# Score matmuls ahead of the later tasks' row-maximum pieces in TensorE's attention slots

## The chip, the cores and the metric

The kernel runs on one core of one Trainium2 chip. The metric is the device time of one execution in microseconds (us), the median of the runs shown. Lower is better.

## The reference, cut to what matters

One transformer block over 1024 positions of width 1024, all in float32. A normed input is projected once. Four branches mix the positions: a gated short convolution, sparse attention, causal pooling and a spatial gating unit. Their outputs are gated and merged, an output projection and a residual follow, and a gated feed-forward layer with a short convolution ends the block. The change lies in the attention branch. Cut to that branch, for each tile of 128 queries:

```python
sc = einsum('bqgrd,bngd->bqgrn', qb, kc) * scale      # compressed keys (63 of them)
pc = softmax(where(cval, sc, NEG));   o_c = pc @ vc
ss_ = einsum('bqgrd,bqgkd->bqgrk', qb, ksel) * scale  # selected blocks: all 16 are selected here
ps = softmax(where(smask, ss_, NEG)); o_s = ps @ vsel
sw = einsum('bqgrd,bkgd->bqgrk', qb, kwb) * scale     # window of the last 512 positions
pw = softmax(where(wmask, sw, NEG));  o_w = pw @ vwb
o = gt[..., 0:1] * o_c + gt[..., 1:2] * o_s + gt[..., 2:3] * o_w
```

There are 8 heads of 64 channels in 2 groups of 4 heads. The heads of a group share keys and values. The top 16 of 16 key blocks are taken, so the selected branch is plain causal attention.

## The kernel before, in words

The kernel is one program with five instruction streams (SyncE for the transfers, GpSimd, ScalarE, VectorE, TensorE), written out by hand and tied together by counting semaphores. Nothing reorders the work: each engine executes what its block in `build` issues, in that order. After the input norm, a loop over the two groups (`GROUPS`) does first the projection of q, k and v for eight tiles of 128 positions and then the attention of the group. The other branches, the merges, the output projection and the feed-forward layer follow, all of them built from 128x512 matmuls with operands split into a high and a low part (L1617 to L1619, L1765).

**Tasks, units and pieces.** `attention_tasks` makes 24 tasks per group: tiles 7 down to 0, and for each tile one task of kind "slc", one "win", one "cmp". A task's keys are cut into units of 128 keys (`units`, 74 in a group). The softmax of a query needs its row maximum first, and that maximum is computed by a pass of its own. `attention_pieces` cuts each task's score rows into pieces of at most 512 columns (77 in a group). For a piece, TensorE's `rows` computes rough scores with the queries on the partitions: one 128-row matmul for each head (L1519), followed by a short bf16 matmul that adds the mask where the piece holds a diagonal or a window edge or is of kind "cmp" (L1521). The pieces alternate between banks 0 and 1, so `rows` waits until VectorE has reduced the piece before the last (`max_done`). VectorE takes the maximum (L1095, written to `nmx`); for a task with over 512 keys it joins two halves (L1100). When the last piece of a task is reduced, GpSimd builds `shift`, a diagonal matrix of the negated maxima (L627).

**Units.** `scores` computes a unit with the keys on the partitions and all four heads in 512 columns: high keys (L1541), low keys (L1542), a mask where needed (L1544) and the broadcast of the maxima (`ones` against `shift`, L1546). It waits for `shift` at the first unit of a task, and for the exponential of the unit before the last (`exp_done`). ScalarE then makes `pT` by Exp (L753) and its high part (L756), VectorE the low part `pT_l` (L1087), and `values` multiplies with the values, three matmuls with 65-column weights (L1562 to L1564), in a slot that is `LAG` = 3 later.

**After a task's last unit.** ScalarE evacuates the sum (`oT`, L762), TensorE turns it (L1590, slot "turn"), and VectorE divides and gates it (`wtmp`, L1114; `wgt`, L1118; `o_gated`, L1121). After the third task of a tile GpSimd adds the three branches (L636, L638, slot "sum"), TensorE transposes the result (L1599, slot "final"), and ScalarE and VectorE write it as a high and a low part (L767, L1129).

**Slots.** `attention_slots` lays this out in 81 slots, one unit each. It places a piece up to `MAXIMA` - 1 = 3 tasks and up to `LEAD` = 12 positions ahead. Slot 0 holds the eight pieces of task 0, slot 11 holds nine (tasks 2 and 3), and most others hold none, one or two. All four compute engines walk the same list `slots`, each with its own order inside a slot. VectorE's order: the reductions of the slot's pieces, the low part of the unit of the slot before, the work of a turn, the work of a final. ScalarE's: exponential and high part, evacuation, final. GpSimd's: the shift of a task whose last piece stands in the slot, then a sum. TensorE's order inside a slot, which the change touches, is at L1569 to L1603: a step of the key compression in slots 0 to 3, 6 and 10, then `rows` for all pieces, `scores`, `values`, turn, final.

Of the kernel before, what the change touches and what calls it, by code (L numbers as in the profile page):

```python
# [101 lines left out]
def after(eng, semaphore, base, n):  # L102


    if n > 0:
        eng.wait_ge(semaphore, base + n)
# [71 lines left out]
def build(nc, x, norm1_g, w_in, conv_a_w, qk_norm_g, cmp_pe, cmp_w1, cmp_w2, pool_w, pool_scale,  # L178
# [13 lines left out]
    with ExitStack() as ctx:  # L192
# [1218 lines left out]
        def _(pe):  # L1411
# [19 lines left out]
            with pe.Fori(0, GROUPS) as g:  # L1431
# [41 lines left out]
                def compressed(step, part=None):  # L1473

                    if step == 0:
                        if part == 0:

                            pe.wait_ge(cbias_done, g + 1)

                        j = part // 2  # L1480
                        for l in range(part % 2 * (L16 // 2), (part % 2 + 1) * (L16 // 2)):
                            ins = nc.tensor.matmul(bank[0:HD, 7, j * HD:j * HD + NCMP], w1[:, j, l, :],
                                                   kcT[:, j, l:l + CMP_STRIDE * (NCMP - 1) + 1:CMP_STRIDE],
                                                   start=l == 0, stop=l == L16 - 1)
                    elif step == 1:

                        pe.wait_ge(compress_act, g * 3 + 1)
                        pe.wait_ge(const2_loaded, 32)
                        pe.sem_inc(passed, 1)
                        for j in range(2):  # L1490
                            ins = nc.tensor.matmul(bank[0:NCMP, 7, 256 + j * HD:256 + (j + 1) * HD], h1[:, j, 0:NCMP],
                                                   w2[:, j, :], start=True, stop=True)
                    else:
                        pe.wait_ge(compress_dve, g * 3 + 3)
                        pe.sem_inc(passed, 1)
                        for a in range(2):
                            ins = nc.tensor.transpose(bank[:, 7, 384 + a * CW:384 + a * CW + NCMP],
                                                      ckd[0:NCMP, a, :, :].rearrange("n u d -> n (u d)"), ident[0:NCMP,
                                                              0:NCMP])
                    if part is None or part == 3:  # L1500
                        ins.then_inc(compress_pe, 1)

                def rows(at, n, r0, heads, c, w):


                    i, kind, k0, keys, blocks = tasks[n]
                    after(pe, max_done, g * PIECES, at - 1)
                    masks = []
                    if kind == "cmp":
                        masks.append((0, CW, cmask[:, i, :]))  # L1510
                    else:
                        if kind == "win" and i >= WIN // P and c == 0:
                            masks.append((0, P, wstart[:, :]))
                        if c + w == keys:
                            masks.append((w - P, P, tri[:, :]))
                    for r in range(heads):
                        o = bank[:, at % 2, r * w:(r + 1) * w]
                        kh = kcAB[:, 0, :] if kind == "cmp" else kAB[:, 2 * (kind == "win"), k0 + c:k0 + c + w]
                        ins = nc.tensor.matmul(o, qT[:, r0 + r, i * P:(i + 1) * P], kh, start=True, stop=not masks)  # L1519
                        for m, (a, mw, mask) in enumerate(masks):  # L1520
                            ins = nc.tensor.matmul(o[:, a:a + mw], identb[:, :], mask, start=False, stop=m == len(masks) - 1)  # L1521
                    ins.then_inc(rows_done, 1)

                def scores(u, n, j):

                    i, kind, k0, keys, blocks = tasks[n]
                    if j == 0:
                        pe.wait_ge(shift_done, g * NT + n + 1)
                    after(pe, exp_done, g * UNITS, u - 1)
                    q = qT[:, :, i * P:(i + 1) * P]  # L1530
                    if kind == "cmp":
                        pe.sem_inc(passed, 1)
                        nr, kh, kl, mask = CW, kcAB[:, 0, :], kcAB[:, 1, :], cmask[:, i, :]
                    else:
                        nr, at = P, k0 + j * P
                        kh, kl = (kAB[:, 2 * (kind == "win") + a, at:at + P] for a in range(2))
                        mask = tri[:, :] if j == blocks - 1 else None
                        if kind == "win" and i >= WIN // P and j == 0:
                            mask = wstart[:, :]
                    o = bank[0:nr, 3 + u % 2, :]  # L1540
                    nc.tensor.matmul(o, kh, q, start=True, stop=False)  # L1541
                    nc.tensor.matmul(o, kl, q, start=False, stop=False)  # L1542
                    if mask is not None:
                        nc.tensor.matmul(o, mask, identb[:, :].unsqueeze(1).broadcast_to([P, REP, P]), start=False,  # L1544
                                stop=False)
                    nc.tensor.matmul(o, ones[:, 0:nr], shift[:, n % MAXIMA, :, :], start=False,  # L1546
                            stop=True).then_inc(s_done, 1)

                def values(u, n, j):

                    i, kind, k0, keys, blocks = tasks[n]
                    pe.wait_ge(ptl_done, g * UNITS + u + 1)
                    if j == 0:
                        after(pe, evac_done, g * NT, n - 1)
                    pe.sem_inc(passed, 1)
                    if kind == "cmp":
                        nr, vh, vl = CW, vc_h[:, :], vc_l[:, :]
                    else:
                        ty = 0 if kind == "slc" else 1
                        nr, vh, vl = P, v_h[:, ty, k0 // P + j, :], v_l[:, ty, k0 // P + j, :]  # L1560
                    o = bank[0:HD + 1, 5 + n % 2, :]
                    nc.tensor.matmul(o, vh, pT_h[0:nr, u % RING, :], start=j == 0, stop=False)  # L1562
                    nc.tensor.matmul(o, vh, pT_l[0:nr, u % RING, :], start=False, stop=False)  # L1563
                    nc.tensor.matmul(o, vl, pT_h[0:nr, u % RING, :], start=False, stop=j == blocks - 1).then_inc(pv_done, 1)  # L1564
# [5 lines left out]
                for slot in slots:  # L1570
                    if slot["n"] <= COMPRESS[0]:
                        compressed(0, slot["n"])
                    elif slot["n"] in COMPRESS:
                        compressed(COMPRESS.index(slot["n"]))
                    if slot["n"] == COMPRESS[2] + 1:
                        pe.wait_ge(compress_act, g * 3 + 3)
                    for piece in slot["pieces"]:
                        rows(*piece)
                    if slot["unit"]:
                        scores(*slot["unit"])  # L1580
                    if slot["values"]:
                        values(*slot["values"])
                    if slot["turn"] is not None:

                        n = slot["turn"]
                        pe.wait_ge(evac_done, g * NT + n + 1)
                        after(pe, gated, g * NT, n)
                        pe.sem_inc(passed, 1)
                        for r in range(REP):
                            ins = nc.tensor.transpose(bank[:, 7, r * (HD + 1):(r + 1) * (HD + 1)],  # L1590
                                                      oT[:, n % 2, r * P:(r + 1) * P], ident[0:HD + 1, 0:HD + 1])
                        ins.then_inc(turned, 1)
                    if slot["final"] is not None:

                        i = slot["final"]
                        pe.wait_ge(summed, g * TT + i + 1)
                        after(pe, ol_done, g * TT, i)
                        for b in range(2):
                            ins = nc.tensor.transpose(bank[:, 2, b * P:(b + 1) * P],  # L1599
                                                      o_gated[:, 3 * i % 4, b * P:(b + 1) * P], ident[:, :])  # L1600
                        ins.then_inc(final_done, 1)
# [204 lines left out]
```

## Time and profile before

| what | us |
|---|---|
| median of 3 runs | 2223.41 |
| lowest and highest of them | 2220.38, 2224.12 |
| span of the profiled execution, first to last instruction | 2220.0 |
| TensorE matmul busy in it | 2124.8 (96%) |
| VectorE, ScalarE, GpSimd busy | 1001.7, 668.0, 108.5 |
| mean granted TensorE clock | 0.974 |
| attention slots of group 0, of group 1 (from the first row piece to the last transpose) | 126.9 to 308.9, 397.7 to 580.4 |

The profile is of one execution, on one core. The record of it gives its span and no total of its own beside it; the nearest total is the lowest run, 0.4 us above the span. Times in the rows are microseconds from the span's start. A matmul's duration in a timeline is its start to its modelled end and overlaps the next one's, so the pace is read from start to start. "PEld" is the loading of weights, which runs beside the matmuls. "PEclk" is the share of the full TensorE clock (2.4 GHz) that was granted: 1.00 or 0.50, or a mean of both over a stretch.

### The profile page before, as it was taken

What the parts mean: (1) busy time and instruction counts of PE and PEld (TensorE: products, weight loads), DVE (VectorE), ACT (ScalarE), POOL (GpSimd) and SP (SyncE); (2) the same over time, 40 slices, a digit from 0 to 9 for tenths busy, and PEclk for the clock granted to TensorE, in tenths of its full rate; (3) what the DMA queues carried; (4) which work ended last, traced back from release to release, by engine and by line L of the source; (5) the groups of instructions that cost most, each with busy time, mean ns of one, the idle gap of its engine ahead of it and who ended that gap; (6) DMA issues with size and microseconds to landing.
All of it is one profiled execution on the core that took longest, in us unless ns stands there. A gap on an engine that the chain in (4) does not pass through costs nothing.

```text
span 2220.0 us, 27176 instructions
## 1 busy us (share of the span) xinstructions
PE 2124.8 (96%) x10106; PEld 1717.7 (77%) x10106; DVE 1001.7 (45%) x1543; ACT 668.0 (30%) x970; POOL 108.5 (5%) x109
## 2 busy tenths in 40 slices
PE   4989979799899999999999999999999999999998
PEld 3956659566588888888788888878888888888886
DVE  6647756477323323234533432544443444344443
ACT  4446644466422111122312322422111122111111
POOL 1002320023100000000000000000000000000000
PEclk6979989799999999999999999999999999999999
DMA  6010000000112111121211111502111111101111
GB/s 167 1 39 1 1 17 1 1 1 1 30 43 57 48 53 43 43 62 43 57 48 52 29 53 51 171 1 86 42 35 57 47 47 57 57 28 47 54 41 76
DMA packets 148135, 99.03 MB, mean 45 GB/s; under 512 B 22203, under 2 KB 139661, under 8 KB 148045
## 3 DMA queue, kind: packets, MB, share of 16 engines
q1 hardware_dynamic: 147805, 97.07, 14.9%
q8 instruction: 54, 0.88, 0.2%
q0 software_dynamic: 240, 0.79, 0.1%
q14 instruction: 36, 0.29, 0.0%
HBM read 93.64 MB, written 4.19 MB: 44 GB/s over the span
## 4 chain that ended last, share of the span: by engine, by line
PE 92%; DVE 4%; ACT 2%; issue 2%; POOL 1%; DMA 0%; SPq 0%; DVEq 0%; ACTq 0%; POOLq 0%; PEldq 0%
PE bank L1617 18%; PE bank L1618 18%; PE bank L1619 18%; PE bank L1765 11%; PE bank L1719 4%; PE bank L1519 2%; PE bank L1541 2%; PE bank L1546 1%; PE bank L1562 1%; PE bank L1542 1%; PE bank L1564 1%; PE bank L1563 1%; PE bank L1456 1%; PE bank L1460 1%; PE bank L1458 1%
## 5 line engine op out<-in xcount | busy, mean ns | idle before, releaser
L1617 PE MATMUL bank<-actT_h,ring_h 128*128 128x512 f32 x1536 | 599.4, 390 | 8.8 <-DVE actT_l L1353 4.8
L1619 PE MATMUL bank<-actT_h,ring_l 128*128 128x512 f32 x1536 | 598.5, 390 | 0.0
L1618 PE MATMUL bank<-actT_l,ring_h 128*128 128x512 f32 x1536 | 598.4, 390 | 0.0
L1617 PEld LDWEIGHTS bank<-actT_h,ring_h 128*128 128x128 f32 x1536 | 288.8, 188 | 69.9 <-issue 7.8
L1619 PEld LDWEIGHTS bank<-actT_h,ring_l 128*128 128x128 f32 x1536 | 288.7, 188 | 60.0
L1618 PEld LDWEIGHTS bank<-actT_l,ring_h 128*128 128x128 f32 x1536 | 288.8, 188 | 59.4
L1136 DVE TENSOR_TENSOR ring_l<-raw,ring_h 128x1024 fp32r<-128x1024 f32 x128 | 156.4, 1222 | 353.0 <-ACT ring_h L783 352.7
L783 ACT ACTIVATE ring_h<-raw 128x1024 fp32r<-128x1024 f32 x128 | 134.7, 1053 | 142.1 <-PE bank L1619 124.8
L1365 DVE TENSOR_TENSOR x<-x,bank 128x1024 f32<-128x1024 f32 x88 | 107.4, 1221 | 100.7 <-PE bank L1765 99.5
L940 ACT ACTIVATE ffa_h<-ffc 128x1024 fp32r<-128x1024 f32 x22 | 23.3, 1061 | 341.4 <-DVE ffc L1397 341.4
L753 ACT ACTIVATE pT<-bank 128x512 f32<-128x512 f32 (+1 forms) x148 | 88.1, 595 | 117.6 <-PE bank L1546 114.0
L1095 DVE TENSOR_REDUCE nmx<-bank 128x1 f32<-128x512 f32 (+4 forms) x154 | 95.5, 639 | 60.7 <-PE bank L1521 47.1
L1087 DVE TENSOR_TENSOR pT_l<-pT,pT_h 128x512 fp32r<-128x512 f32 (+1 forms) x148 | 104.4, 706 | 24.9 <-ACT pT_h L756 24.7
L1765 PE MATMUL bank<-wd_h,ffa_h 128*128 128x512 f32 x352 | 109.3, 392 | 3.7 <-DVE ffa_l L1399 3.7
L1765 PE MATMUL bank<-wd_l,ffa_h 128*128 128x512 f32 x352 | 108.9, 391 | 0.0
L1765 PE MATMUL bank<-wd_h,ffa_l 128*128 128x512 f32 x352 | 108.8, 391 | 0.0
L1617 PE MATMUL bank<-outb_h,ring_h 128*128 128x512 f32 x256 | 100.4, 392 | 2.5 <-DVE outb_l L1230 2.5
L1619 PE MATMUL bank<-outb_h,ring_l 128*128 128x512 f32 x256 | 100.4, 392 | 0.0
L1618 PE MATMUL bank<-outb_l,ring_h 128*128 128x512 f32 x256 | 100.2, 391 | 0.0
L756 ACT ACTIVATE pT_h<-pT 128x512 fp32r<-128x512 f32 (+1 forms) x148 | 93.5, 631 | 4.7
L1380 DVE TENSOR_SCALAR ffc<-ffg,chan 128x1024 f32<-128x1024 f32 x22 | 16.6, 754 | 163.4 <-ACT ffg L927 163.4
L627 POOL TENSOR_TENSOR shift<-ident,nmx 128x512 fp32r<-128x512 f32 x48 | 63.7, 1328 | 394.3 <-DVE nmx L1100 255.0
(303 smaller groups left out, 2993.2 us busy)
## 6 DMA issues: line engine op xcount, KB each, us to landing
raw<-in_w_in SPq DMA_DIRECT2D x60, 512.0 KB, 3.7
raw<-in_w_up SPq DMA_DIRECT2D x44, 512.0 KB, 3.9
wd_raw<-in_w_down SPq DMA_DIRECT2D x22, 512.0 KB, 5.2
raw<-in_w_branch SPq DMA_DIRECT2D x32, 256.0 KB, 2.7
x_in<-in_x SPq DMA_DIRECT2D x8, 512.0 KB, 8.1
raw<-in_w_o SPq DMA_DIRECT2D x8, 512.0 KB, 3.5
x<-in_x SPq DMA_DIRECT2D x8, 512.0 KB, 10.1
out<-x SPq DMA_DIRECT2D x8, 512.0 KB, 2.6
```

What stands on the lines that cost most here:

```text
L753: nc.scalar.activation(pT[0:nr, u % RING, :], bank[0:nr, 3 + u % 2, :], ACT.Exp).then_inc(exp_done, 1)
L756: nc.scalar.activation(pT_h[0:nr, u % RING, :], pT[0:nr, u % RING, :], ACT.Copy).then_inc(pth_done, 1)
L783: nc.scalar.activation(ring_h[:, slot, :], raw[:, slot, :], ACT.Copy).then_inc(ph_done, 1)
L1087: nc.vector.tensor_tensor(pT_l[0:nr, u % RING, :], pT[0:nr, u % RING, :], pT_h[0:nr, u % RING, :].bitcast(F32), ALU.subtract).then_inc(ptl ...
L1095: nc.vector.tensor_reduce(nmx[:, n % MAXIMA, c // HALF, r0:r0 + heads], bank[:, at % 2, 0:heads * w].rearrange("p (r n) -> p r n", r=heads ...
L1136: nc.vector.tensor_tensor(dst, src, hi.bitcast(F32), ALU.subtract).then_inc(pl_done, 1)
L1365: nc.vector.tensor_tensor(x2[:, t, :], x2[:, t, :], flat[:, (2 + t % 2) * 1024:(3 + t % 2) * 1024], ALU.add).then_inc(d_done, 1)
L1617: nc.tensor.matmul(o, wh(k), ah[:, k, cols], start=k == 0, stop=False)
L1618: nc.tensor.matmul(o, wh(k), al[:, k, cols], start=False, stop=False)
L1619: ins = nc.tensor.matmul(o, wl(k), ah[:, k, cols], start=False, stop=k == k_tiles - 1)
L1719: ins = nc.tensor.matmul(bank[:, first_bank + h, :], m, w[:, h * HALF:(h + 1) * HALF], start=k == 0 and n == 0, stop=k == KT - 1 and n == 2)
L1765: ins = nc.tensor.matmul(o[h], av, w[:, k, h * HALF:(h + 1) * HALF], start=k == 0 and n == 0, stop=k == 1 and n == 2)
```

## The change

In each slot, TensorE's list of pieces is parted in two. Pieces of the task that the slot's own unit belongs to stay ahead of `scores`. Pieces of a later task are issued after `scores` and ahead of `values`. The other engines' programs are unchanged, and so are the semaphores, the buffers and the instructions themselves.

```diff
@@ -1574,10 +1574,14 @@
                     if slot["n"] == COMPRESS[2] + 1:
                         pe.wait_ge(compress_act, g * 3 + 3)
+                    later = [p for p in slot["pieces"] if slot["unit"] and p[1] > slot["unit"][1]]
                     for piece in slot["pieces"]:
-                        rows(*piece)
+                        if piece not in later:
+                            rows(*piece)
                     if slot["unit"]:
                         scores(*slot["unit"])
+                    for piece in later:
+                        rows(*piece)
                     if slot["values"]:
                         values(*slot["values"])
                     if slot["turn"] is not None:
```

By the slot list, the eight pieces of slot 0 stay where they are (they are of task 0, as its unit is), and the other 69 pieces of a group, in 50 slots, move behind their slot's `scores`.

## Rows read from the trace of the kernel before

**Rows 1.** The page, part 1: busy time of each engine, share of the span, instructions.
```profile
PE 2124.8 (96%) x10106; PEld 1717.7 (77%) x10106; DVE 1001.7 (45%) x1543; ACT 668.0 (30%) x970; POOL 108.5 (5%) x109
```
**Rows 2.** A window of group 0's attention: length, busy time and instructions by engine, clock, DMA.
```profile
172.00:280.00 108.00, 107.31 (x578) 69.70 (x576) 79.03 (x160) 73.79 (x127) 32.04 (x27) 1.00 0.00 1
```
**Rows 3.** Waits of TensorE's matmuls, whole span: us in total, times, longest.
```profile
PE bank L1599 <- POOL o_gated L638: 8.0, 6, 2.8
...
PE bank L1541 <- ACT pT L753: 6.0, 2, 3.0
...
PE bank L1541 <- POOL shift L627: 4.2, 2, 2.1
...
PE bank L1519 <- DVE nmx L1095: 2.6, 12, 0.4
```
**Rows 4.** Timeline of VectorE in slot 11, group 0: start, us, instruction, idle before.
```profile
165.87 5.33 DVE L1095 TENSOR_REDUCE nmx<-bank 128x4 f32<-128x256 f32 x9 [1.43 <-PE bank L1521]
```
**Rows 5.** Timeline of TensorE at the start of slot 22, group 0.
```profile
193.01 0.40 PE L1519 MATMUL bank<-kAB,qT 128*128 128x512 f32 x1
193.24 0.23 PE L1521 MATMUL bank<-wstart,identb 128*128 128x128 bf16 x1
193.28 0.48 PE L1541 MATMUL bank<-qT,kAB 128*128 128x512 f32 x1
```
**Rows 6.** Lines L1541 and L1562: duration in ns, least, median, most.
```profile
L1541 PEld LDWEIGHTS bank<-qT,kAB x132: 186/200/354, 135.5 to 567.3; 128*128 128x128 f32 x132
L1541 PE MATMUL bank<-qT,kAB x132: 389/474/797, 135.5 to 567.3; 128*128 128x512 f32 x132
L1541 PEld LDWEIGHTS bank<-qT,kcAB x16: 135/148/153, 175.1 to 568.8; 128*64 128x64 f32 x16
L1541 PE MATMUL bank<-qT,kcAB x16: 387/424/430, 175.1 to 569.0; 128*64 128x512 f32 x16
...
L1562 PEld LDWEIGHTS bank<-pT_h,v_h x132: 134/136/229, 148.0 to 572.8; 128*65 128x65 f32 x132
L1562 PE MATMUL bank<-pT_h,v_h x132: 387/392/632, 148.2 to 572.8; 128*65 128x512 f32 x132
```
**Rows 7.** Timelines of three engines from slot 70 to the final of slot 71.
```profile
290.19 0.28 PE L1519 MATMUL bank<-kcAB,qT 128*128 128x64 f32 x1
...
290.82 0.43 PE L1541 MATMUL bank<-qT,kcAB 128*64 128x512 f32 x1
...
292.04 0.40 PE L1562 MATMUL bank<-pT_h,v_h 128*65 128x512 f32 x1
...
295.29 0.44 PE L1599 MATMUL bank<-ident,o_gated 128*128 128x128 f32 x2 [0.51 <-POOL o_gated L638]
...
291.48 0.42 DVE L1095 TENSOR_REDUCE nmx<-bank 128x4 f32<-128x256 f32 x1 [0.22 <-issue]
...
292.07 1.34 POOL L627 TENSOR_TENSOR shift<-ident,nmx 128x512 fp32r<-128x512 f32 x1 [3.27 <-DVE nmx L1095]
```
**Rows 8.** Timelines from slot 62 to the final of slot 64.
```profile
273.23 1.28 DVE L1095 TENSOR_REDUCE nmx<-bank 128x2 f32<-128x512 f32 x2
...
275.37 0.66 DVE L1118 TENSOR_TENSOR wgt<-wtmp,glog 128x4 f32<-128x4 f32 x1
...
274.67 1.34 POOL L627 TENSOR_TENSOR shift<-ident,nmx 128x512 fp32r<-128x512 f32 x1 [4.78 <-DVE nmx L1095]
...
278.87 0.33 PE L1599 MATMUL bank<-ident,o_gated 128*128 128x128 f32 x1 [0.69 <-POOL o_gated L638]
```
**Rows 9.** The sum and the final of tile 7 (slots 18 and 19).
```profile
187.21 1.06 POOL L638 TENSOR_TENSOR o_gated<-o_gated 128x256 f32<-128x256 f32 x1
...
188.58 0.38 PE L1599 MATMUL bank<-ident,o_gated 128*128 128x128 f32 x2
```
**Rows 10.** Windows of slots 11 to 13 in either group; columns as in Rows 2.
```profile
165.12:177.03 11.91, 10.98 (x53) 6.21 (x52) 10.46 (x20) 4.17 (x8) 2.49 (x2) 1.00 0.00 1
435.37:448.87 13.50, 12.56 (x53) 7.15 (x52) 10.30 (x20) 4.17 (x8) 2.49 (x2) 0.87 0.00 1
```

## The prediction

> **What bounds the kernel now.** I read four views, from coarse to fine. The page says that TensorE's matmuls are busy for 96% of the span and VectorE for 45% [rows 1], so the first question is whether the attention slots are different. The window over the middle of group 0's attention answers it: 107.31 us of matmuls in 108.00 us, at full clock, with VectorE at 79.03 and ScalarE at 73.79 us [rows 2]. Through most of the slots the path is TensorE's own list of matmuls. Giving another engine its input sooner can only pay where TensorE waits for that engine. The waits of the whole span name these places [rows 3]: 6.0 us for an exponential at L1541, 4.2 us for a shift at L1541, 2.6 us for the maxima at L1519, 8.0 us for GpSimd's branch sum at L1599. A difference under about 0.2% (4.4 us) can't be told from no change.
>
> **None of the waits that scores could shorten lies at a moved piece.** The 6.0 us for an exponential are two waits, one in each group. Both stand in slot 8, behind table loads and the compression steps on ScalarE, and slots 4 to 10 hold no piece. The two shift waits (4.2 us) are slot 0, whose eight pieces stay in front. So what the new order gives ScalarE, an exponential that starts earlier by the pieces' time, saves nothing: I cost it at 0, and what covers it is the dense list of TensorE. The waits for maxima stand in the runs of eight or nine pieces. In slot 11 VectorE reduces nine pieces in 5.33 us without a gap [rows 4], and TensorE follows it at that pace through two banks. With scores in front, the run starts later by the length of scores and ends later by the same, and the slot's sum of times is the same: 0. Neither order puts the scores inside the run. No instruction is added or dropped, no DMA is issued in these slots, and no wait is new; only the order of waits on TensorE differs.
>
> **Term 1, what follows a mask matmul.** A 512-column matmul starts 0.23 us before the next instruction [rows 5]. The short mask matmul after it starts only 0.04 us before L1541, but then L1541 lasts long: 474 ns in the median where a value matmul after a long one lasts 392 [rows 6]. The 82 ns are the loading of 128 weight columns, which a short matmul doesn't hide. Where the scores are of kind "cmp" and have 64 columns of weights, the load takes 148 ns, not 200, and the matmul 424, so 32 ns stick out [rows 6]. In the new order a masked piece is followed not by scores but by values, whose weights have 65 columns and load in 136 ns [rows 6]. By the nearest row (64 columns) that leaves 32 of 82 ns and saves 0.05 us. By the slot list, 31 slots of each group have a masked last piece, scores that aren't "cmp", and values that aren't either. That is 62 x 0.05 = 3.1 us saved. The bounds: nothing saved, if the values' first load sticks out as far as the scores' did (0), and all of it hidden, 62 x 0.082 = 5.1 us.
>
> What stood before the pieces (values, or the transposes of a turn) now stands before scores, with weights of the same 128 columns: 0. In the 7 slots of a group with "cmp" scores the saving is missing and a 128-column load follows their last matmul. I take 0.03 us each, 14 x 0.03 = 0.4 us lost, between 0 and 14 x 0.082 = 1.1 us. The eight slots of each group whose last piece has no mask, and slots 1 and 2 (no values yet): 0.
>
> **Term 2, later reductions.** What moves behind scores reaches VectorE later by the time of three score matmuls, 3 x 0.23 + 0.08 = 0.77 us. VectorE runs in order, so the low part and the turn's division queue behind the late reduction. The low part is needed three slots on; values have over 1.6 us in hand everywhere, by the timelines, and that covers it: 0. The tight chain is another: turn, division and gate on VectorE, sum on GpSimd, final on TensorE, within two slots. TensorE waits at three finals of each group, six times in all [rows 3]. The last stands behind all pieces and isn't touched. One by one, in group 0:
>
> - Final of slot 71. Its sum stands on GpSimd behind the shift of the last piece. That piece is computed from 290.19 to about 291.0 and reduced from 291.48, the shift starts at 292.07, and TensorE stands idle 0.51 us ahead of 295.29 [rows 7]. The "cmp" scores take 292.04 - 290.82 = 1.22 us [rows 7]. With them in front the piece ends at 292.2, is reduced from 292.3 instead of 291.48, and shift, sums and final come later by the same 0.85 us.
> - Final of slot 64. The reductions of slot 62 start at 273.23 because VectorE is free only then [rows 8]; with the pieces 0.77 us later they start at about 273.8. Then low part, division and gate: 0.6 us, on a final that already waits 0.69 us [rows 8].
> - Final of slot 19. The sum ends at 188.27, the final starts at 188.58 [rows 9], so 0.3 us are in hand. VectorE is about 0.35 to 0.4 us later after two turns in a row: 0.1 us.
> - The other finals have from 0.4 to 1.0 us in hand, or stand behind slots without pieces: 0.
>
> That is 1.55 us a group, 3.1 us in all. Lower bound: 0, if VectorE's lateness is made up. Upper bound: the full 0.77 us at all eight finals and 1.22 at slot 71's, less the 0.3 and more in hand, some 2.9 us a group, 5.8 us.
>
> Here a rule speaks against the change. In slot 62 VectorE's `wgt`, four values a partition, takes 0.66 us and ends at 276.03, and GpSimd's shift runs from 274.67 to 276.01 [rows 8]: the small one stood behind the big one. The Trainium skill says the same (SBUF — State Buffer, "Who interferes with whom"): a VectorE instruction with two SBUF inputs and a GpSimd instruction that reads SBUF take a shared port pair in turns, and the loser waits for the whole instruction. The trace agrees in this slot. Later shifts fall onto the gating more often by that rule, and the sum would be at the upper bound of term 2, not at 3.1.
>
> **Sum.** -3.1 + 0.4 + 3.1 = +0.4 us on the profiled execution (span 2220.0, no total of its own). It lies 0.4 us under the lowest run and 3.4 under the median, 2223.41; I put the difference on the median: 2223.8.
>
> **The rivals.** *Clock.* In group 1 the slots 11 to 13 take 13.50 us at a mean clock of 0.87, in group 0 11.91 at 1.00 [rows 10], same instructions. The nine paced pieces leave TensorE with gaps, and in group 1 it fell to half clock (1.2 GHz) behind them. The change moves dense scores from behind to ahead of the gaps, so either group can fall or not: -1.6 to +1.6 us, within the range, no sign. It widens each case.
>
> *Faster.* The mask term comes out at its bound (-5.1), the finals lose little because TensorE's savings and VectorE's catching up cancel (+1), and group 1 keeps its clock (-1.6): 2223.4 - 5.7 = 2217.7. For it: the weight loads of rows 6. Against it: the 64-column row shows 32 ns left, and rows 7 show a chain without any reserve. It needs over 4.4 us in all. 0.08.
>
> *Slower.* VectorE and GpSimd turn into the bound at the finals. Place: turn to final; price: the 0.77 us of scores at each final, 5.8 us in all as above. For it: rows 7 and 8, two finals with no reserve. Against it: four of the other finals have 0.4 us or more in hand. It decides if the mask term stays under about 1 us at the same time: +5.8 + 0.4 - 0.5 = +5.7, so 2229.1. 0.09.
>
> *The order doesn't change.* The slot list excludes it: 69 pieces of 77 move. 0.
>
> **How the numbers follow.** Forecast (mask term and finals cancel within 4 us): 0.83, all within 0.2%. Faster 0.08, slower 0.09. The range takes term 1 and term 2 against each other at about three quarters of their bounds, and 1.6 us of clock either way: -4 to +4 about 2223.6, so 2219.6 to 2227.8, and leaves out most of both rivals.
>
> **What would show it.** Steps: L1541 at 392 ns in the masked slots and L1562 at some 424; the final of slot 71 idle about 1.4 us and that of 64 about 1.3, in both groups; waits at L1541 and L1519 as before; the paced run of slot 11 as long as before, starting behind scores; L1599's waits at about 11 us in all instead of 8.0. I'd be wrong if L1562 after a mask stays at 392 (term 1 at its upper bound) or goes to 474 (no gain), if waits for `pT_l` turn up at L1562, or if all eight finals wait.

## The result, and the profile after

| | before | changed |
|---|---|---|
| median of the 20 runs of each, taken side by side, us | 2221.68 | 2224.57 |
| lowest to highest, us | 2220.11 to 2224.12 | 2222.46 to 2228.21 |
| ratio, 95% interval | | 1.0015 [1.0008, 1.0022] |
| span of the profiled execution, us | 2220.0 | 2224.0 (its own time: 2225.96) |

Two of the 20 runs before took 3466.93 and 3749.08 us; they are slow runs and are left out of the range shown, and the ratio is of fast runs.

The change costs 0.15%, some 3.3 us, by this ratio (2.9 us between the medians). That lies within the range given (2219.6 to 2227.8) and within the 0.2% called "no change", though the interval of the ratio excludes 1. Several lines moved down by four: L1590 is now L1594, L1599 is L1603.

The busy times of the page barely differ, so they explain nothing [rows 1]:

```profile
PE 2125.9 (96%) x10106; PEld 1718.5 (77%) x10106; DVE 1013.4 (46%) x1543; ACT 670.2 (30%) x970; POOL 107.8 (5%) x109
```

The waits of TensorE's matmuls, changed kernel (us in total, times, longest):

```profile
PE bank L1603 <- POOL o_gated L638: 11.8, 6, 2.8
PE bank L1541 <- ACT pT L753: 6.4, 4, 3.0
...
PE bank L1541 <- POOL shift L627: 4.2, 2, 2.1
...
PE bank L1519 <- DVE nmx L1095: 2.4, 11, 0.4
```

Against [rows 3] one line has moved by more than half a microsecond: the finals wait 11.8 us instead of 8.0, still six times. Waits for shifts are the same, those for maxima 0.2 us less, those for exponentials 0.4 us more. The 0.4 are two new waits of 0.19 us (at 150.80 in group 0), ahead of the 3 us wait of slot 8, and no wait for an exponential stands behind slot 8 in either kernel.

The two lines that answer to [rows 6], changed kernel (ns: least, median, most):

```profile
L1541 PEld LDWEIGHTS bank<-qT,kAB x132: 186/188/337, 135.7 to 571.6; 128*128 128x128 f32 x132
L1541 PE MATMUL bank<-qT,kAB x132: 389/397/795, 135.7 to 571.7; 128*128 128x512 f32 x132
...
L1562 PE MATMUL bank<-pT_h,v_h x132: 387/422/669, 148.3 to 577.2; 128*65 128x512 f32 x132
```

The first score matmul fell from 474 to 397 ns. The first value matmul, now the one behind the mask, rose from 392 to 422, not to 474. The same in slot 22, in TensorE's timeline (start, us, instruction), against [rows 5]:

```profile
196.07 0.40 PE L1546 MATMUL bank<-shift,ones 128*128 128x512 f32 x1
196.31 0.39 PE L1519 MATMUL bank<-kAB,qT 128*128 128x512 f32 x1
196.54 0.23 PE L1521 MATMUL bank<-wstart,identb 128*128 128x128 bf16 x1
196.58 0.43 PE L1562 MATMUL bank<-pT_h,v_h 128*65 128x512 f32 x1
196.84 0.39 PE L1563 MATMUL bank<-pT_l,v_h 128*65 128x512 f32 x1
```

Read the starts: from the mask (L1521, 196.54) to the second value matmul (196.84) it takes 0.30 us. In the kernel before, the same slot took 0.36 us from the mask to the second score matmul (193.24 in [rows 5] to 193.60):

```profile
193.60 0.40 PE L1542 MATMUL bank<-qT,kAB 128*128 128x512 f32 x1
```

The saving exists, at 0.05 to 0.06 us a slot. It can be added up over all masked pieces from slot 13 to slot 61 of group 0, 31 of them: from the start of the first matmul behind the mask to the next start it took 9.52 us in all before (medians 0.31 us for scores with 128 columns of weights) and 8.17 us in the changed kernel (0.26 for values). That is 1.35 us less.

What eats it is at the end of the group. Timelines around the final of slot 64, changed kernel:

```profile
280.99 0.44 PE L1603 MATMUL bank<-ident,o_gated 128*128 128x128 f32 x2 [1.27 <-POOL o_gated L638]
...
275.34 1.29 DVE L1095 TENSOR_REDUCE nmx<-bank 128x2 f32<-128x512 f32 x2 [0.43 <-PE bank L1521]
...
277.36 0.79 DVE L1118 TENSOR_TENSOR wgt<-wtmp,glog 128x4 f32<-128x4 f32 x1
...
276.79 1.34 POOL L627 TENSOR_TENSOR shift<-ident,nmx 128x512 fp32r<-128x512 f32 x1 [4.53 <-DVE nmx L1095]
```

In [rows 8] the reductions followed VectorE's own work without a gap; now VectorE waits 0.43 us for the pieces, everything behind them is late, and TensorE's idle time at the final is 1.27 us instead of 0.69. And from slot 68 to the final of slot 71:

```profile
291.80 0.40 PE L1564 MATMUL bank<-pT_h,v_l 128*65 128x512 f32 x1
292.18 0.44 PE L1594 MATMUL bank<-ident,oT 65*128 65x65 f32 x4
292.60 0.41 PE L1541 MATMUL bank<-qT,kcAB 128*64 128x512 f32 x1
...
293.78 0.19 PE L1519 MATMUL bank<-kcAB,qT 128*128 128x64 f32 x1
...
290.82 0.79 DVE L1118 TENSOR_TENSOR wgt<-wtmp,glog 128x4 f32<-128x4 f32 x1
291.65 0.42 DVE L1121 TENSOR_TENSOR o_gated<-bank,wgt 128x256 f32<-128x256 f32 x1
...
294.99 0.42 DVE L1095 TENSOR_REDUCE nmx<-bank 128x4 f32<-128x256 f32 x1 [1.50 <-PE bank L1521]
...
290.25 1.34 POOL L627 TENSOR_TENSOR shift<-ident,nmx 128x512 fp32r<-128x512 f32 x1 [2.34 <-DVE nmx L1095]
295.57 1.34 POOL L627 TENSOR_TENSOR shift<-ident,nmx 128x512 fp32r<-128x512 f32 x1 [3.98 <-DVE nmx L1095]
296.87 1.16 POOL L636 TENSOR_TENSOR o_gated<-o_gated 128x256 f32<-128x256 f32 x1
298.12 0.72 POOL L638 TENSOR_TENSOR o_gated<-o_gated 128x256 f32<-128x256 f32 x1
...
298.89 0.44 PE L1603 MATMUL bank<-ident,o_gated 128*128 128x128 f32 x2 [1.82 <-POOL o_gated L638]
```

Against [rows 7] the idle time ahead of the final grew from 0.51 to 1.82 us. A third place is new: in slot 69 the turn starts 0.38 us after L1564, not 0.23. It has to wait for the gating of slot 68, which ended only at 292.07. Its `wgt` took 0.79 us beside the shift (290.25 to 291.59), where the next one, with no shift beside it, took 0.16.

To compare kernels I cut each group at three matmuls that all versions have. "Slots 0 to 13" runs from the first row piece to the first value matmul of slot 13, "13 to 61" on to that of slot 61, "61 to 71" on to the final of slot 71. In us, worked out from the starts of matmuls, group 0 and group 1:

| kernel | slots 0 to 13 | 13 to 61 | 61 to 71 | to the last final |
|---|---|---|---|---|
| before | 49.41, 50.45* | 94.80, 94.79 | 24.15, 24.15 | 12.95, 12.93 |
| changed | 51.86*, 50.22* | 93.70, 93.68 | 26.15, 26.07 | 13.15, 13.01 |

The star (in the stages below too) marks a stretch in which the clock fell to half after it had risen; every group begins at half clock, until 138 to 141 us in group 0, before and after the change alike. The middle of a group gains 1.1 us, its end loses 2.0, in both groups alike. The third difference is the clock in slots 0 to 13. Windows over that part of group 0, first of the kernel before (columns as in Rows 2):

```profile
126.00:165.00 39.00, 31.81 (x151) 20.49 (x150) 18.05 (x40) 19.91 (x32) 2.49 (x2) 0.81 0.23 47
160.00:176.00 16.00, 13.79 (x66) 7.96 (x64) 13.19 (x32) 7.29 (x13) 2.49 (x2) 1.00 0.00 1
```

and of the changed kernel:

```profile
126.00:165.00 39.00, 33.06 (x146) 21.12 (x145) 17.38 (x39) 19.73 (x30) 2.49 (x2) 0.72 0.24 49
160.00:176.00 16.00, 15.25 (x55) 9.15 (x54) 10.90 (x27) 6.32 (x12) 2.48 (x2) 0.74 0.00 0
```

TensorE ran at half clock (1.2 GHz) for 6.8 us from 158.1 and for 3.4 us from 171.7; the kernel before had neither in this group. The first fall begins inside the 3 us wait for an exponential in slot 8, which both kernels have [rows 3]; that slot holds no moved piece. TensorE's timeline there, changed kernel:

```profile
159.04 0.79 PE L1541 MATMUL bank<-qT,kAB 128*128 128x512 f32 x1 [2.99 <-ACT pT L753]
```

The matmul behind the wait lasts 0.79 us instead of some 0.40, which is half clock in one row. The two profiles differ by 4.0 us of span: 2.4 in slots 0 to 13 of group 0, -0.2 in those of group 1, -2.2 in the middle stretches, +3.9 in the late ones, +0.3 in the tails, and -0.2 elsewhere. So the order itself makes +1.7 us in these two traces (-2.2 and +3.9).

### The profile page after: what moved, and what is told of

Same layout as the page of the kernel before. It is cut to its first block, busy times and chain, and to the rows that moved or that the text cites. A ratio compares the mean times of both kernels' runs of the same rounds, so it can differ in the third digit from the quotient of the medians.

```text
span 2224.0 us, 27176 instructions
## 1 busy us (share of the span) xinstructions
PE 2125.9 (96%) x10106; PEld 1718.5 (77%) x10106; DVE 1013.4 (46%) x1543; ACT 670.2 (30%) x970; POOL 107.8 (5%) x109
## 3 DMA queue, kind: packets, MB, share of 16 engines
HBM read 93.64 MB, written 4.19 MB: 44 GB/s over the span
## 4 chain that ended last, share of the span: by engine, by line
PE 92%; DVE 4%; ACT 2%; issue 2%; POOL 1%; DMA 0%; DVEq 0%; SPq 0%; ACTq 0%; POOLq 0%; PEldq 0%
PE bank L1621 18%; PE bank L1622 18%; PE bank L1623 18%; PE bank L1769 11%; PE bank L1723 4%; PE bank L1519 2%; PE bank L1541 2%; PE bank L1546 2%; PE bank L1562 1%; PE bank L1542 1%; PE bank L1564 1%; PE bank L1563 1%; PE bank L1456 1%; PE bank L1460 1%; PE bank L1458 1%
## 5 line engine op out<-in xcount | busy, mean ns | idle before, releaser
L1087 DVE TENSOR_TENSOR pT_l<-pT,pT_h 128x512 fp32r<-128x512 f32 (+1 forms) x148 | 111.2, 759 | 16.3 <-ACT pT_h L756 16.0
```

The source lines that it names most:

```text
L1087: nc.vector.tensor_tensor(pT_l[0:nr, u % RING, :], pT[0:nr, u % RING, :], pT_h[0:nr, u % RING, :].bitcast(F32), ALU.subtract).then_inc(ptl ...
```

## The experiments

My theory was that of the prediction: masks ahead of values save some 0.05 us each, and late reductions cost that and more at the finals of slots 64 and 71. There were two rivals. One was that the clock makes the difference, and that where the early pieces stand decides whether it falls. The other was that something in the early scores themselves, not in the late pieces, makes the time.

**First four: parts of the change.** All have the changed kernel's code; only the condition for `later` differs.

e1, slots 62 and on in the old order:

```diff
-later = [p for p in slot["pieces"] if slot["unit"] and p[1] > slot["unit"][1]]
+later = [p for p in slot["pieces"] if slot["unit"] and p[1] > slot["unit"][1] and slot["n"] < 62]
```

> The new order in slots 0 to 61, the old one from slot 62 on. Theory A (the loss is the chain reduction, division, branch sum, final at slots 62 to 71): the two late finals of each group wait 0.69 and 0.51 us again instead of 1.27 and 1.82, TensorE's wait at the transposes of slot 69 goes too, and what the weight loads behind masks save stays. The stretch from slot 14 to the final of slot 71 is about 1.3 us shorter than before in each group, the whole about 2.5 us under before (2219) and over 4 us under the changed kernel. Rival B (the loss is half clock behind slots 8 to 13, which the new order brings on more often): the time stays at that of the changed kernel, some 2224, with the falls of the clock in place.

Measured: median 2221.67 (2217.77 to 2224.61, 11 runs), ratio 0.9996 [0.9987, 1.0005]. Stages 49.12, 49.02 | 93.66, 93.72 | 24.17, 24.18. Its two finals in group 0:

```profile
277.16 0.44 PE L1603 MATMUL bank<-ident,o_gated 128*128 128x128 f32 x2 [0.70 <-POOL o_gated L638]
293.59 0.44 PE L1603 MATMUL bank<-ident,o_gated 128*128 128x128 f32 x2 [0.51 <-POOL o_gated L638]
```

The whole late loss is gone and the middle gain stays. The median isn't the 2219 that was expected: only 4 of the 11 runs lie at 2217.8 to 2218.6, the others at 2220.8 and up. The profiled run, with no fall of the clock in slots 0 to 71, has a span of 2218.9. It's one of the slower ones, and its trace shows where the time went: outside the attention, in parts that no version changes, it took 2.8 us more than the kernel before. Behind the last final it took 1642.2 us to the end, where the kernel before took 1639.7, with half clock from 1082.3 and from 1485.1, 3.4 us each; the kernel before had one such stretch, from 1086.1.

e2, the opposite: only slots 62 and on in the new order.

```diff
+... and slot["n"] >= 62]
```

> The old order in slots 0 to 61, the new one from slot 62 on. Theory A: the whole loss of the chain without the saving, 2 x 2.2 us minus some 0.2 us for the three masked pieces there, so +4.2 us against before (2225.9). Rival B (the clock in the early slots): same as before, within 1 us.

Measured: 2227.30 (2225.70 to 2231.24, 8 runs), ratio 1.0024 [1.0013, 1.0034]. Stages 49.35, 50.39* | 94.80, 94.80 | 26.11, 26.07. The loss stands alone, without the gain: 1.95 us a group in slots 61 to 71, 3.9 us in all. The median lies higher than that and than the 2225.9 expected; its profile shows one more fall of the clock, at 297 us, in the tail of group 0 (14.47 us instead of 12.95).

e3, the change everywhere but in slot 70:

```diff
+... and slot["n"] != 70]
```

> The new order everywhere but in slot 70, whose one piece goes ahead of the scores again. Theory A with the last piece as its main part: the final of slot 71 waits about 0.5 us instead of 1.82, 1.3 us less in each group, 2.6 us under the changed kernel; the final of slot 64 still waits 1.27. Rival C (the final of slot 71 is late because VectorE is late from slot 68 on, not because of the piece of slot 70): the wait at slot 71 stays over 1.2 us.

Measured: 2223.46 (2220.32 to 2225.79, 11 runs), ratio 1.0003 [0.9994, 1.0012]. Stages 50.23*, 51.78* | 93.61, 93.68 | 24.79, 24.76. GpSimd and TensorE at the final of slot 71 (two timelines):

```profile
291.27 1.34 POOL L627 TENSOR_TENSOR shift<-ident,nmx 128x512 fp32r<-128x512 f32 x1 [2.70 <-DVE nmx L1095]
292.57 0.73 POOL L636 TENSOR_TENSOR o_gated<-o_gated 128x256 f32<-128x256 f32 x1
293.38 1.06 POOL L638 TENSOR_TENSOR o_gated<-o_gated 128x256 f32<-128x256 f32 x1
...
294.50 0.44 PE L1603 MATMUL bank<-ident,o_gated 128*128 128x128 f32 x2 [0.56 <-POOL o_gated L638]
```

One piece of 77 carries two thirds of the loss: moving it back takes the stage from 26.1 to 24.8, 1.3 us a group. Of the 2.6 us that this should save in all, the medians show 1.1; this trace has both falls of the clock in group 1. The final of slot 64 still waits 1.26 us, which with the turn of slot 69 is the other third.

e4, slots 1 to 13 in the old order, the change in the rest:

```diff
+... and slot["n"] > 13]
```

> The old order in slots 0 to 13, the new one behind them. Theory A: waits at the finals as in the changed kernel, the time within 1 us of it plus 0.3 us (three masked slots lose their saving). Rival B: the falls of the clock behind slots 8 to 13 go back to what they are before, and the time comes down by 1.5 to 3 us, to about 2222.

Measured: 2224.18 (2222.68 to 2227.45, 11 runs), ratio 1.0013 [1.0004, 1.0022]. Stages 52.40*, 50.39* | 93.66, 93.58 | 26.06, 26.09. It is as slow as the changed kernel, and its clock fell at 157.6 and 171.3 us, as there, though slots 0 to 13 are issued as before. The new order of the early pieces isn't needed for those falls. Whether it makes them more frequent, the run times don't tell.

**Second four: the rivals, and better orders.**

e5, pieces of later tasks behind `values` instead of ahead of them:

```diff
-                    for piece in later:
-                        rows(*piece)
                     if slot["values"]:
                         values(*slot["values"])
+                    for piece in later:
+                        rows(*piece)
```

> The later tasks' pieces stand behind values instead of between scores and values. The exponentials start as early as in the changed kernel, but a mask matmul is no longer followed by the values' 65-column weights. Theory A1 (slots 14 to 60 got shorter by 1.1 us a group because of the weight loads): from the values of slot 13 to those of slot 61 the time goes back to about 94.8 us, and L1541 back to about 474 ns. Rival D (they got shorter because scores and exponentials are early): it stays at 93.7. The finals wait longer than in the changed kernel, the pieces being a further 0.69 us later: some 3 us a group from there to the final of slot 71; the whole about 2228.

Measured: 2245.07 (2238.93 to 2245.58, 4 runs), ratio 1.0104 [1.0090, 1.0119]. Stages 49.41*, 49.29* | 98.08, 98.06 | 28.62, 28.65 | 14.49, 14.49. Lines of its waits, and of L1541:

```profile
PE bank L1603 <- POOL o_gated L638: 15.5, 10, 2.8
...
PE bank L1594 <- issue: 4.0, 10, 1.0
```

```profile
L1541 PE MATMUL bank<-qT,kAB x132: 387/476/795, 134.4 to 582.1; 128*128 128x512 f32 x132
```

The expectation (94.8 us for the middle, 2228 in all) was far too low. Scores are as early here as in the changed kernel, but the pieces reach VectorE another 0.7 us later, and the loss follows their lateness: ten finals wait, turns wait too, and the middle stretch, which gained in the changed kernel, loses 3.3 us a group. The mask now stands before scores or a turn again, and L1541 is back at 476 ns. So the mask term goes away with the order, as expected. The middle stretch can't say whether early scores are worth something by themselves, because the late pieces cost more than that. The traces of before and changed say it: no wait for an exponential stands in that stretch in either, so there was nothing for earlier scores to shorten, and the 1.35 us at the masks are more than the 1.1 gained. The median lies 6 us above the profiled run, which is the fastest of the four; that part has no explanation here.

e7, as e1, and GpSimd adds the branches (slot "sum") ahead of the shift of the same slot; only slot 70 has both:

```diff
                 for slot in slots:
-                    for at, n, r0, heads, c, w in slot["pieces"]:
-                        if at + 1 == piece_end[n]:
...
                     if slot["sum"] is not None:
...
                         nc.gpsimd.tensor_tensor(o[0], o[0], o[2], ALU.add).then_inc(summed, 1)
+                    for at, n, r0, heads, c, w in slot["pieces"]:
+                        if at + 1 == piece_end[n]:
...
```

> The new order in slots 0 to 61 only, and GpSimd adds the branches (sum) ahead of a shift that stands in the same slot, which is so in slot 70 alone. Theory A: the final of slot 71 was waiting because its sum stood behind the last shift, so its wait goes to about 0: a further 0.5 us less in each group than with the new order up to slot 61 alone; undisturbed runs at about 2217, 4 us under before. Rival: the shift that is later by then holds up the scores of slot 73, and nothing is gained.

Measured: 2218.54 (2217.64 to 2220.00, 11 runs), ratio 0.9985 [0.9977, 0.9994]. Stages 50.25*, 50.18* | 93.70, 93.64 | 23.51, 23.48. GpSimd, and TensorE at the final of slot 71:

```profile
290.08 0.72 POOL L623 TENSOR_TENSOR o_gated<-o_gated 128x256 f32<-128x256 f32 x1 [2.54 <-DVE o_gated L1121]
290.88 1.06 POOL L625 TENSOR_TENSOR o_gated<-o_gated 128x256 f32<-128x256 f32 x1
291.90 1.04 POOL L635 TENSOR_TENSOR shift<-ident,nmx 128x512 fp32r<-128x512 f32 x1
...
293.35 0.39 PE L1603 MATMUL bank<-ident,o_gated 128*128 128x128 f32 x2
```

The sum is ready at 291.94, the final stands in TensorE's list at 293.35: no wait. The shift, which the sum had stood behind, is needed later still, and no new wait for a shift turns up (4.2 us, twice, as before). By the stage this is worth 0.7 us a group over e1. This kernel is 0.15% faster than the kernel before, and 6 us faster than the changed one by the medians.

e8, only slots 1 to 13 in the new order (`and slot["n"] <= 13`):

> The new order in slots 0 to 13 only. Theory A: within 0.6 us of before, slightly faster (0.1 to 0.3 us a group). Rival B (the early slots bring more falls to half clock): more than half of the runs have a mean clock under 0.973 or between 0.976 and 0.980 and are 3 to 4 us longer, as in the kernels with the new order in the early slots, and the median is 1.5 us or more over before.

Measured: 2221.83 (2220.55 to 2227.77, 12 runs), ratio 1.0006 [0.9998, 1.0015]. Stages 50.12*, 48.98 | 94.85, 94.84 | 24.18, 24.17. The new early order alone costs nothing that can be told. Three of the 12 runs lie at 2227.3 to 2227.8, at a lower mean clock; no trace shows where it fell.

e9, from the kernel before: the pieces stay in front, and `values` go ahead of `scores` in the slots without turn or evacuation (37 a group, 25 of them with a masked last piece), so that masks stand before values and no reduction is late:

```diff
+ahead = slot["values"] and slot["turn"] is None and slot["evacuate"] is None
+if ahead: values(*slot["values"])
 if slot["unit"]:
     scores(*slot["unit"])
-if slot["values"]:
+if slot["values"] and not ahead:
     values(*slot["values"])
```

> From the kernel before: the pieces stay in front, and in slots without a turn or an evacuation values go ahead of scores (pieces, values, scores). Theory A1: a masked piece is followed by the values' weights as in the changed kernel, in 25 slots of a group, and no reduction is late: 1.1 us less in each group before slot 61, the finals wait as before (0.69 and 0.51), and 0.7 us of the wait of slot 8 is filled by values. About 3.5 us under before, 2218 in undisturbed runs. Rival E (scores that are 0.69 us later starve ScalarE, and values wait for its low parts): waits at L1562 or L1590 of over 1 us a group, and no gain.

Measured: 2223.60 (2220.69 to 2225.88, 11 runs), ratio 1.0005 [0.9996, 1.0014]. The expected 2218 was missed by over 5 us. In group 1, where the clock didn't fall again, start to final of slot 71 took 167.50 us against 168.36 in group 0 of the kernel before (its group without a fall), 0.86 us less. I had put 1.8 on it. Seen by stages, slots 0 to 13 gain (47.99), 13 to 61 lose (95.72 against 94.79) and 61 to 71 gain (23.79). So with this order the mask term shows only in part; where the 0.9 us lost in the middle stretch come from stays open.

**Last three: the clock.** The traces of the changed kernel, e3 and e4 show half clock from inside the 3 us wait of slot 8, and their run times fall into shorter and longer ones. So I filled that wait, and the one of slot 10, in three kernels: f1 is the kernel before, f2 the changed one, f3 is e7, each with matmuls in slots 8 and 10 whose results nothing reads:

```diff
+for _ in range({8: 12, COMPRESS[2]: 5}.get(slot["n"], 0)):
+    nc.tensor.matmul(bank[:, 2, :], kAB[:, 0, 0:P], qT[:, :, 0:P], start=True, stop=True)
```

> The kernel before, with 12 matmuls of 512 columns into an unused bank ahead of the scores of slot 8 and 5 ahead of the compression step of slot 10, in each group. They fill the waits of 3.0 and 1.3 us there and compute nothing that is read. Theory F (the runs that are 3 to 4 us longer have a fall to half clock that the waits of slots 8 and 10 bring on, in either order, by a few tenths of a us of displacement): those runs all but vanish, the fastest runs stay where they are (2220.5 to 2221.5), the median comes down by under 1 us. Rival: the falls come from the paced pieces of slot 11, and their share stays.

> The changed kernel with the same filling. Theory F: nearly all runs lie at 2222.5 to 2224, where the undisturbed half of its runs lies, so the median comes down from 2224.6 to about 2223.3, and 2.0 us over the filled kernel before are left, which are the late finals minus the weight loads. Theory B (the order itself brings the falls on): half of the runs still lie at 2226.

> The new order up to slot 61, the old one behind, the sum ahead of the shift in slot 70, and the same filling. If the terms add up: 2217.5 to 2218.5 in nearly all runs, 3 to 4 us under before.

| kernel | median | lowest, highest | ratio to before | 13 to 61 | 61 to 71 |
|---|---|---|---|---|---|
| f1 | 2220.72 | 2220.05, 2222.88 | 0.9999 [0.9990, 1.0008] | 94.82, 94.82 | 24.19, 24.18 |
| f2 | 2223.07 | 2222.69, 2226.61 | 1.0010 [1.0001, 1.0019] | 93.64, 93.64 | 26.18, 26.09 |
| f3 | 2217.59 | 2216.10, 2218.59 | 0.9982 [0.9973, 0.9991] | 93.64, 93.61 | 23.48, 23.50 |

The window of f2 that answers to 0.74 above, and a line of f3's waits that answers to 6.4 us:

```profile
160.00:176.00 16.00, 14.95 (x71) 8.85 (x70) 12.61 (x30) 7.39 (x14) 2.49 (x2) 1.00 0.01 2
```

```profile
PE bank L1541 <- ACT pT L753: 0.9, 4, 0.2
```

With the wait filled, group 0 keeps its full clock there, and the difference of changed and before is 2223.07 - 2220.72 = 2.35 us. By the intervals of the two ratios that is uncertain by about 2 us; the stages of these two traces give +1.5 for the order (-2.4 and +3.9). f3 is 3.1 us faster than f1 and 5.5 faster than f2, and is the fastest kernel of all.

## Why the prediction was right, point by point

The sum said +0.4 us. The stages of the traces say +1.7 for the order, the filled pair +2.35, and the medians of 20 runs +2.9. The change came out inside "within 0.2%", by terms of the right kind: a small gain and a somewhat larger loss, the loss sized too small, with a clock term on top. That the number itself came so near (2223.8 put, 2224.57 measured) is partly luck. It was put on the median of three runs, 2223.41, and the median of 20 is 1.7 us lower; that error and the 2.5 us missing from the sum work in opposite directions. The range was written about 2223.6 and up to 2227.8, where -4 to +4 gives 2227.6; nothing hangs on it.

**What costs nothing.** Right. Waits at L1541 for shifts and at L1519 for maxima are as before within 0.2 us, none turned up at `pT_l`, and early scores by themselves brought nothing (no wait for an exponential stands behind slot 8, and e8). "No wait is new" wasn't quite right: two waits of 0.19 us for an exponential and the one at the turn of slot 69 are.

**Term 1, masks before values: -3.1 us, less 0.4 for "cmp" slots.** Right in mechanism, and about right in size. The count left out two masked slots a group whose values are "cmp" (41 and 68); they change nothing here. L1541 and L1562 came out at 397 and 422 ns where 392 and "some 424" were put. The middle stretch alone gained 1.1 us a group (1.35 at the masks, less 0.25 elsewhere): 93.58 to 93.72 us in the seven kernels that have the new order there, 94.79 to 94.85 in the four that have the old one. e1 kept it with the late slots undone. In slots 0 to 13 the traces without a fall vary from 49.41 before to 48.98 and 49.25 in others, so what is gained there can't be told apart. In slots 62 to 70 TensorE waits for the chain anyway, and savings ahead of a wait are only more wait. So of 2.7 us net about 2.2 to 2.7 came in.

**Term 2, late reductions: +3.1 us.** The mechanism and the two main places were right, the size wasn't: +2.0 us a group instead of 1.55. In group 0, in time rather than in idle time of TensorE, the changed kernel is 0.52 us later from the values of slot 61 to the final of slot 64 (8.25 us, 7.73 before), 0.29 from there to the first matmul of slot 70 (11.61, 11.32 before) and 1.19 from there to the final of slot 71 (6.29, 5.10 before). The waits grew by somewhat more, because TensorE is earlier at them by its saved loads. Piece by piece:

- Final of slot 64: the wait grew by 0.58, as put (+0.6).
- Final of slot 71: +1.19 in time, and +1.31 in the wait, instead of +0.85. The step that failed is "the piece ends at 292.2, is reduced from 292.3". From the last mask matmul of this piece to the start of its reduction it takes 0.69 us in the kernel before and 0.70 in the changed one:

```profile
290.79 0.20 PE L1521 MATMUL bank<-cmask,identb 128*128 128x64 bf16 x1
...
294.29 0.21 PE L1521 MATMUL bank<-cmask,identb 128*128 128x64 bf16 x1
```

  The reductions start at 291.48 and 294.99. I took it that in [rows 7] VectorE was the late one, with slack to use up. It was free at 291.26 and waited for the piece, so there was no slack. From the first matmul of the piece to the final it takes 5.10 us before and 5.11 in the changed kernel: the chain passes on the whole 1.18 us of the "cmp" scores put in front of it. The reduction began 1.21 us after the piece's start, where I had allowed 0.89; that is 0.3 of the 0.46 missing in the wait. The rest, about 0.1 us each, is TensorE coming earlier to the final and the sum on GpSimd, which took 1.97 us from 296.87 where it took 1.87 before.
- Turn of slot 69: +0.15, and another 0.15 to the scores behind it (0.42 us after the turn's start, 0.27 behind other turns), not foreseen. The gating stood behind the shift. Here the rule weighed in the prediction acted: by the Trainium skill (SBUF — State Buffer, "Who interferes with whom") a VectorE instruction with two SBUF inputs and a GpSimd instruction that reads SBUF contend for a shared port pair, which is an exclusive lock. The trace agrees: `wgt` took 0.79 us beside a shift and ended with it (291.61, the shift 291.59), 0.16 without. It explains one new wait in slot 69, not the upper bound of term 2.
- Final of slot 19: 0.1 was put, nothing came. Its sum ended at 191.16, and the final started at 191.21 without a wait.
- The upper bound, all finals: wrong. Six waits before, six after.

**The clock: -1.6 to +1.6 us, no sign.** The clock gave a term, but the place was wrong in part, and in the profiled pair it was larger than the bound (+2.4 us in slots 0 to 13 of group 0, -0.2 in group 1). I looked at slots 11 to 13, behind the nine paced pieces. The fall behind them exists, and over slots 0 to 13 it costs about 1.1 us where 1.6 was put: they took 50.0 to 50.5 us with it alone and 49.0 to 49.4 with none (e5 and e9, whose order differs more, left aside). The longer and more costly stretch starts in slot 8, in a 3 us wait that neither order touches; with both falls those slots took 51.8 to 52.4 us. By the mean granted clock the runs fall into shorter and longer ones (0.974, 0.975 or from 0.981 up against 0.969 to 0.973 or 0.978 to 0.980). Of the changed kernel 10 of 20 were of the longer kind, and 7 of 30 of the kernel before in one comparison; such runs took some 3 us more (in e8, 6). That is as much as the clock term needs, the 1.2 us between the medians that terms 1 and 2 leave of the 2.9, but it isn't shown to be this term: a mean doesn't say where the clock fell. The trace of e1 is of the longer kind and has no fall in slots 0 to 71, and e2's has one at 297 us, in the tail. Outside the attention, where all kernels do the same, the 13 traces differ by up to 3.2 us.

What the traces do show is that the early order isn't needed for the fall in slot 8: e4 has the old order and falls. In the ten kernels that weren't filled, the 3 us wait stands 20 times, and the clock fell inside it in three of them (the changed kernel, e3, e4). Filling the wait goes with fewer runs of the longer kind: f1 and f3 none of 11, f2 three of 11. Each pair alone is too few runs to tell from chance; together it's 3 of 33 against 19 of 61 in the unfilled three. Why the unfilled kernels differ so, from 2 of 11 in e7 to 11 of 11 in e9, stays open. That small shifts of where the wait falls decide it is argued, not shown.

**The rivals.** The faster one needed finals at +1 us and failed on them. The slower one had its place right, turn to final, but only two of the eight finals lost; e2 shows the loss without the gain, 1.0024.

## What to carry to other kernels

Moving work later in a saturated in-order list is free only if nobody downstream is tight: follow it through every in-order engine to the next wait of the saturated one, and read the slack from the start of the producer to the start of the consumer, not from the gap ahead of the consumer. A gain of 1.1 us a group was real and could be kept by undoing the change in its last five slots alone (e1), and another 0.7 us a group came from putting the instruction that releases the wait at the end ahead of one that nobody needed yet (e7). Where the clock falls in a known wait, matmuls that fill it may make the times steadier: the 11 runs of f1 lie within 2.8 us and those of f2 within 3.9, where 27 unfilled runs of the kernel before spread over 4.6 and 20 of the changed one over 5.8.

## What the runs showed of the hardware that was not expected

- What a weight load costs behind a short matmul differs with the load. With 65 columns the first value matmul takes 0.26 us from its start to the next (0.23 behind a long matmul), with 128 columns the first score matmul 0.31 (again 0.23). Which matmul follows a short one is therefore worth some 0.05 us each time.
- A 3 us wait of TensorE at full clock was followed by half clock in some traces and not in others of the same wait. With that fall (6.8 us at half clock) and the later one of 3.4 us, slots 0 to 13 took 51.8 to 52.4 us; with the later one alone 50.0 to 50.5; with none 49.0 to 49.4.
- A four-element VectorE instruction with two inputs took 0.16 us, or 0.79 beside GpSimd's 1.34 us shift. GpSimd's 128x256 add took from 0.72 to 1.16 us; the longest stood beside two `pT_l` of VectorE.
- From the last short mask matmul of a "cmp" piece to the start of VectorE's reduction it took 0.69 and 0.70 us, with VectorE free: a chain has such a step even where no engine is busy.
